# Attention probabilities scaled on GpSimd instead of VectorE, in a one-core transformer block kernel

## The reference, cut to what matters

```python
def masked_softmax(s, mask):
    s = jnp.where(mask, s, NEG)
    m = jnp.max(s, axis=-1, keepdims=True)
    e = jnp.where(mask, jnp.exp(s - m), 0.0)
    return e / jnp.maximum(jnp.sum(e, axis=-1, keepdims=True), 1e-30)
...
        p_slc = masked_softmax(s, kpos <= t[:, None])
        o_slc = jnp.einsum('bghqn,bgqnd->bqghd', p_slc.astype(v_sel.dtype), v_sel)
...
        p_win = masked_softmax(s, wmask)
        o_win = jnp.einsum('bghqs,bsgd->bqghd', p_win.astype(v_w.dtype), v_w)
        o = gc[..., 0:1] * o_cmp + gc[..., 1:2] * o_slc + gc[..., 2:3] * o_win
```

## Time and profile before

| | us |
|---|---|
| median of three runs | 2156.81 |
| the profiled execution, its own time | 2157.0 |
| its span, first to last instruction | 2155.2 |
| PE busy | 2020.5 (94%) |
| DVE busy | 1292.8 (60%) |
| ACT busy | 818.2 (38%) |
| POOL busy | 356.8 (17%) |

### The profile page before, as it was taken

One profiled execution on the slowest core, in us unless ns is written; L12 is line 12 of the kernel. 1 busy time (PEld: TensorE's weight loads), 2 busy tenths in 40 slices (PEclk: granted clock), 3 DMA queues, 4 the chain that ended last, 5 costly groups with the idle time before them and its releaser, 6 DMA issues.

```text
span 2155.2 us, 22175 instructions
## 1 busy us (share of the span) xinstructions
PE 2020.5 (94%) x8726; PEld 1544.3 (72%) x8726; DVE 1292.8 (60%) x1837; ACT 818.2 (38%) x1207; POOL 356.8 (17%) x319
## 2 busy tenths in 40 slices
PE   7999999988878899999999899799999897999997
PEld 5888888755534488888887677676788676866886
DVE  5763444668898346655665677914672559435842
ACT  5331333202333543312333348443542365444531
POOL 2000001155333010000001202401201013102102
PEclk9999999988778999999999899899999898999998
DMA  4232232221000144655542122221123222220221
GB/s 180 95 117 82 98 105 90 82 61 64 11 0 1 45 142 155 206 182 168 196 153 68 59 98 85 79 79 40 55 93 98 88 76 77 70 88 29 86 91 59
DMA packets 53175, 196.72 MB, mean 91 GB/s; under 512 B 5968, under 2 KB 6480, under 8 KB 52432
## 3 DMA queue, kind: packets, MB, share of 16 engines
q1 hardware_dynamic: 42912, 159.50, 21.8%
q0 software_dynamic: 7504, 28.58, 4.1%
q10 hardware_dynamic: 2656, 7.23, 1.0%
HBM read 192.14 MB, written 2.10 MB: 90 GB/s over the span
## 4 chain that ended last, share of the span: by engine, by line
PE 80%; DVE 12%; ACT 4%; POOL 1%; DMA 1%; issue 1%; SPq 0%; POOLq 0%; DVEq 0%; ACTq 0%
PE PS L531 79%; DVE AR L1477 2%; DVE AR L1705 2%; DVE AR L1932 2%; DVE HX L1813 1%; DVE WLO L1474 1%; ACT WHI L1021 1%; DVE AR L1801 1%; DVE HNL L1477 1%; DVE TMP L1477 1%; PE PS L726 1%; DMA RAW<-in_w_in 0%; DMA RAW<-in_w13a 0%; ACT HX L1184 0%; DVE AR L1903 0%
## 5 line engine op out<-in xcount | busy, mean ns | idle before, releaser
L531 PE MATMUL PS<-HNH,WHI 128*128 128x512 f32 x1632 | 663.9, 407 | 19.4 <-ACT HNH L1052 13.9
L1474 DVE TENSOR_TENSOR WLO<-RAW,WHI 128x1024 fp32r<-128x1024 f32 (+1 forms) x270 | 369.1, 1369 | 505.7 <-ACT WHI L1021 505.4
L531 PE MATMUL PS<-HNH,WLO 128*128 128x512 f32 x1632 | 644.7, 395 | 21.6 <-DVE WLO L1474 21.6
L1021 ACT ACTIVATE WHI<-RAW 128x1024 fp32r<-128x1024 f32 (+1 forms) x270 | 296.0, 1097 | 730.1 <-PE PS L531 643.9
L531 PE MATMUL PS<-HNL,WHI 128*128 128x512 f32 x1632 | 438.0, 391 | 0.2
L531 PEld LDWEIGHTS PS<-HNH,WHI 128*128 128x128 f32 x1632 | 311.1, 191 | 103.7 <-issue 23.9
L531 PEld LDWEIGHTS PS<-HNH,WLO 128*128 128x128 f32 x1632 | 311.5, 191 | 96.1 <-DVE WLO L1474 23.0
L531 PEld LDWEIGHTS PS<-HNL,WHI 128*128 128x128 f32 x1632 | 307.9, 189 | 66.3 <-DVE HNL L1477 2.1
L531 PE MATMUL PS<-AR 128*128 128x512 f32 (+12 forms) x700 | 210.3, 515 | 12.4 <-ACT HX L1184 3.9
L2052 POOL TENSOR_TENSOR ACC<-ACC,SQ 128x512 f32<-128x512 f32 x46 | 62.7, 1363 | 786.7 <-ACT SQ L1036 785.8
L531 PEld LDWEIGHTS PS<-AR 128*128 128x128 f32 (+5 forms) x700 | 99.0, 195 | 91.4 <-issue 58.0
(11 more groups left out here) (293 smaller groups left out, 2504.3 us busy)
## 6 DMA issues: line engine op xcount, KB each, us to landing
RAW<-in_w_in SPq DMA_DIRECT2D x80, 512.0 KB, 3.5
AR<-in_w_ada POOLq DMA_DIRECT2D x48, 512.0 KB, 3.9
RAW<-in_w13a SPq DMA_DIRECT2D x44, 512.0 KB, 3.2
RAW<-in_w13b SPq DMA_DIRECT2D x44, 512.0 KB, 4.1
RAW<-in_w_out SPq DMA_DIRECT2D x40, 512.0 KB, 3.6
RAW<-in_w2a SPq DMA_DIRECT2D x16, 704.0 KB, 4.0
RAW<-in_w2b SPq DMA_DIRECT2D x16, 704.0 KB, 5.4
RAW<-in_w_inA SPq DMA_DIRECT2D x12, 512.0 KB, 3.2
```

The costliest lines, as they stand in the source:

```text
L531: return pe.matmul(o, l, r, start=start, stop=stop, skip_group_check=True)
L1021: act.activation(hi_of(name, i), raw_of(name, i), ACT.Copy).then_inc(*HI.up(name, i))
L1474: dve.tensor_tensor(lo_of(name, i), raw_of(name, i), f32(hi_of(name, i)), S_).then_inc(*LO.up(name, i))
```

## The change

VectorE no longer touches the probabilities in the scale step. After the two reciprocals it multiplies each by the gate, one value for each of 128 queries, and leaves the factor in the fourth column of the small tile ST4. GpSimd has a new step of its own: it waits for the factor and multiplies the tile in place. PE's transposes wait for GpSimd's semaphore instead of VectorE's.

```diff
@@ pe_program, step "flip"
-                        pe.wait_ge(*V.at("scale", i, kind, qt, hf))
+                        pe.wait_ge(*G.at("scale", i, kind, qt, hf))
@@ dve_program, step "scale"
                     for hf in range(2):
-                        x = PB[:, us[hf], 0:P * (qt + 1)]
                         dve.wait_ge(*V.at("sum", i, kind, qt, hf))
-                        dve.tensor_scalar(x, x, ST4[:, us[hf], 2:3], GT[:, qt, 8 * kind + 2 * i + hf:8 * kind + 2 * i + hf + 1],
-                                          M_, M_).then_inc(*V.up("scale", i, kind, qt, hf))
+                        dve.tensor_tensor(ST4[:, us[hf], 3:4], ST4[:, us[hf], 2:3], GT[:, qt, 8 * kind + 2 * i + hf:8 * kind + 2 * i + hf + 1],
+                                          M_).then_inc(*V.up("share", i, kind, qt, hf))
@@ pool_program
+                elif step == "scale":
+                    i, kind, qt = at_
+                    for hf in range(2):
+                        u = (2 * (8 * i + 4 * (kind - 1) + qt) + hf) % 4
+                        x = PB[:, u, 0:P * (qt + 1)]
+                        pool.wait_ge(*V.at("share", i, kind, qt, hf))
+                        pool.tensor_scalar(x, x, ST4[:, u, 3:4], None, M_).then_inc(*G.up("scale", i, kind, qt, hf))
```

## The result

The changed kernel takes 2169.23 us, the median of four runs (2167.60 to 2173.80), against 2156.24 for the kernel before. The ratio is 1.0064 [1.0048, 1.0079], which is 13.8 us; the two medians differ by 13.0. Differences of whole kernels are given by the ratio from here on. The prediction said 2153, at most 2165.

A forecast was written before the change was run, and what follows sets the result against it. VectorE was taken to bound the stage's middle stretch (587 to 686.4 us), PE the stretches before and behind. Terms -5.1 - 1.0 + 2.4 = -3.7 us gave 2153 us, range 2141 to 2165.

The forecast's parts named there:

- Part 4: New GpSimd scalings of the eight waiting pairs in the middle: 0.86 us per 512 columns, 8.5 us, net +5.5 us.
- Rival B: GpSimd scaling takes about 2 us per 512 columns, costing tail and queue: 2168, or 2160 at 1.6 us; chance 0.23.
- part 3: Middle, eight pairs waiting for GpSimd: almost none of 19.8 us kept; GpSimd's gaps shrink by 60%, -6.5 us.
- Part 5: Last stretch (tail): three 512-wide pairs ready 0.6 to 1.0 us later a half, narrower pairs at nothing: +2.4 us.
- Part 1: VectorE in the middle loses L1813 and gains 128x1 products at about 0.2 us a pair: 24.8 us gross.
- sign of being wrong: On VectorE: the new 128x1 products blocked so that they cost more than 0.5 us a pair.
- sign of being right: In the middle, L1705, L1477 and L1711 grow by some 10 to 15 us while L1813's 28.05 are gone.
- Part 2: Middle, eight pairs among scans whose scaling did not wait for GpSimd: all 5.1 us of gain kept.
- Part 6: Before 587 us, where PE is the bound: two waiting pairs hide, 0 us (-2 to +1).

The follow-up runs named there:

- sixteen items: Items 6 to 21 scaled on GpSimd, the other 16 on VectorE, against the kernel before: 2158.08 us, ratio 1.0021.

## Why the prediction was wrong

The forecast was -3.7 us; the stage measured +12.2. Half of the miss lies in the tail (+9.8 against +2.4), half in the first part (+2.4 against -6.1). By its own steps:

**Part 4, the price of the GpSimd scaling, is the step that failed.** It took 0.86 us for 512 columns, from the affine select and the time that L2164 held VectorE up. It is 1.55. The upper bound of 2.05, L2164 itself, was the nearer one: the same opcode, type and width. The select is another operation, and held-up time on another engine says how far the two exclude each other, not how long the instruction runs. Rival B named 1.3 us as the point from which it decides, and 1.55 lies beyond it. With 1.55 in its place the prediction's own sum turns round: the eight queued pairs cost 16 x (0.27 + 288 x 0.0025) = 15.8 us instead of 8.5, which makes part 3 and 4 +6.3, and the tail gives three times 2.2, so -5.1 + 6.3 + 6.6 = +7.8 us. This term is 11.5 of the 15.9 us of the miss; the rest is in the parts below.

**Part 5, the tail, was right in place and mechanism, and too small even at the right price.** Half 1 of a 512-wide pair is ready 3.2 us after its scaling could start instead of 1.0; three such pairs make 6.6 us. By the chain, from the last exponential of each of the three items until its transposes are through, the three passes take 13.6 us instead of 5.6, 8.0 more. Another 1.9 are the 18 matmuls at half the clock behind the first of them, shown above. The narrower pairs, which the part cost at nothing, do cost nothing beyond that (8.0 + 1.9 is already all of the 9.8). What the part had left out is the clock: 4.9 of the 9.8 us are PE's own busy time at 0.87 instead of 0.95, partly inside the three passes. In two kernels idle time of PE came with about as much more busy time or somewhat less: 4.9 with 4.9 here, 2.7 with 1.6 with half of each pair on VectorE. Rival B's +9.5 came out near the measured value partly by luck: it had the clock at nothing, a price of 2.05, and 0.7 us for each 384-wide pair.

**Part 1: the 128x1 products.** A quiet pair costs 0.23 us as said; behind the drive products 1.36. In the first part all 44 take 13.8 us, 0.63 a pair on the mean, more than the 0.5 that the prediction had named as a sign of being wrong. So VectorE won 22.7 us with L1813 gone and paid some 5 of them in other lines, where the prediction's sign of being right was 10 to 15.

**Part 2, the quiet items,** held in sign and kept 3.6 of 5.1 us. Their scaling (3.1 us for a 512-wide pair) is longer than the maxima that were to hide it (1.5 us for a pair), and PE waited for it; that this is where the 1.5 us went is likely and not shown.

**Part 3, the queued items.** That nothing of the 21.4 us stays was right (+0.6 by itself, against -1.0). The reason was only partly right. Without the scaling the scans do stretch, from 21.7 us to 24.8 in 582 to 692. In the changed kernel the same 48 scans take 20.8 us: VectorE is no longer the bound, and waits for PE's scores. Behind the fourth product of the recurrence's output (items 5 to 21) the chain of before has 22.6% of L1813, 15.2% of the scans and 15.3% of PE's L531; that of the changed kernel has 34.0% of L531, 13.0% of L2097 and 2.0% of the scans. It goes round through PE, VectorE and GpSimd, and a scaling late in GpSimd's queue delays all three. These pairs measured +0.6 us by themselves, and the corrected sum under part 4 has them at +6.3: it mends the direction and most of the size, and not each term. GpSimd's idle gaps vanished as forecast, into scalings twice as long as forecast. Nor does the new instruction hold VectorE's scans up for its whole length. Four scans beside a 512-wide pair:

```profile
562.58 1.94 DVE L1705 TENSOR_TENSOR_SCAN AR<-AR 128x128 f32<-128x128 f32 x4
```

and the pair (the same trace, GpSimd):

```profile
561.09 3.27 POOL L2097 TENSOR_SCALAR HX<-HX,AR 128x512 f32<-128x512 f32 x2 [1.95 <-DVE AR L1812]
```

1.94 us against 1.61 alone and 5.60 beside GpSimd's multiplications; four others at 676.90 take 1.92. This bears on the rule of the Trainium skill that the prediction used ("SBUF — State Buffer", section "Who interferes with whom", that the two exclude each other entirely): the two-input multiplications agree with it, the one-input scaling does not in this trace. It fits with this that the memsets, which read nothing, cost nearly as much as the working instruction (4.75 of 5.8 us).

**Part 6, the front,** can't be called wrong: +0.4 us by itself, and some 1.4 on the mean, in a part that spreads by 3. Nothing was free there, though: up to the fourth product of the recurrence's output the changed kernel took 112.5 us, and the one whose GpSimd scaling nobody waits for 106.8. So waiting for the results costs as much there as VectorE's relief brings.

The total, from the runs: the scalings off VectorE without any cost -12.7 in the first part, GpSimd's time +5.8, waiting for its results +9.3; in the tail -2.9, +1.6 and +11.1, of which the +1.6 is clock. Sum +12.2 us. The clock is inside these terms, and they are differences of single traces.

## What to carry to other kernels

Moving an elementwise step from a full engine to an idle one trades busy time for latency: where two items are in flight and the next product stands behind this one, count the time until the result is ready, in every stage that the step runs in, also the one where the first engine was never full. Price an instruction that the trace doesn't show by its nearest opcode, type and width, however unwelcome, and look at each idle engine: ScalarE at half the latency won 9.7 us where GpSimd lost 13.8. Split such a move by stage before judging it; here it gained in eight items, did nothing clear in fourteen and lost 10 us in the last ten. And look at what unchanged code does from trace to trace before you read a difference of a few us: a subtraction of three such numbers made an interaction of 4 us that the traces don't show.

## What the runs showed of the hardware that was not expected

**TensorE's clock behind the stage.** The code behind the first OL product is the same in all kernels, yet it took from 1421.2 us (before) to 1428.8 (all on ScalarE) in the profiled executions. Part of it lies in one stretch between two loads of ScalarE's tables, with the same work at another granted clock. The kernel before:

```profile
1348.50:1446.70 98.20, 84.23 (x395) 65.91 (x395) 53.76 (x51) 40.50 (x64) 25.57 (x15) 0.93 0.26 86
```

All on ScalarE:

```profile
1341.30:1442.90 101.60, 86.67 (x393) 66.56 (x392) 53.72 (x51) 40.48 (x63) 25.55 (x15) 0.90 0.25 83
```

3.4 us longer at 0.90 instead of 0.93. A time saved in the stage thus need not be found in the whole: 14.7 us saved in the stage's trace went with 9.7 by the ratio (ScalarE up to item 21), 7.7 with 4.1 (all on ScalarE), and 3.1 with -4.5 (sixteen items). Here one trace stands beside medians, and that of the kernel before has the shortest time behind the stage of all 14, so part of the gap is chance. What puts the clock in one or the other course was not isolated. For differences of some 5 us the stage's own length in the trace says more than the total, within the 3 us that it spreads itself.

**GpSimd's tensor_scalar** in fp32 with one scalar per partition takes 0.27 us and 0.32 for each 128 columns, 1.55 us at 512. The estimate in the prediction from the Trainium skill, "GPSIMD Engine Reference", section 4.1 ("roughly line-rate"), was 0.43 us; the measurement decides, and it is 3.6 times that.

**A pair of 128x1 products can cost 1.36 us.** It does so beside a two-input GpSimd instruction of 1.26 us, and 0.23 without one: the width of a two-input VectorE instruction doesn't protect it.
